# Where ScalarE scales the attention probabilities in the first mixer's loop, and what stands ahead of the copies

## The chip, the cores and the metric

The kernel is one program on one core of a Trainium2 chip. A core has five engines that each run their own list of instructions in order: TensorE (PE) multiplies and transposes, VectorE (DVE) and ScalarE (ACT) do elementwise work, GpSimd (POOL) helps, and SyncE (SP) issues the DMAs. They wait for each other by semaphores. The metric is the time of one execution in microseconds (us) on the device; smaller is better.

## The reference

Two blocks of two layers each run one after the other on 256 latent and 256 context tokens of width 1024. Only the mixer of the very first layer is touched. It joins two branches: a gated linear recurrence in two directions (four heads) and softmax attention (eight query heads, two key heads, 64 wide):

```
def _softmax_attend(q, k, v):
    s = jnp.einsum('bhgqd,bhkd->bhgqk', q, k, preferred_element_type=jnp.float32) * (ATT_HEAD_DIM ** -0.5)
    p = jax.nn.softmax(s, axis=-1).astype(v.dtype)
    return jnp.einsum('bhgqk,bhkd->bhgqd', p, v)
...
    o_lat = jnp.concatenate([a_lat, b_lat], axis=-1)
...
            w_out = even_w_out[j]
...
        x_lat = x_lat + m_lat[2] * _rms(o_lat @ w_out, norm_post_mix[l])
```

Latent queries see all 512 keys, context queries only the 256 context keys.

## The kernel before

The stage `Even` first projects the tokens, then runs a loop of 20 steps (`self.steps`). Each engine has its own copy of that loop (`pe`, `act`, `dve`), with the pieces of several pipelines written out by hand in the order in which that engine is to run them. Three pipelines are interleaved.

**Attention.** There are 16 units: four pairs of heads times four blocks of 128 queries. Unit t is started at step t + 2. Blocks 0 and 1 of a pair are context queries (256 keys wide), blocks 2 and 3 latent ones (512 wide), so units 2, 3, 6, 7, 10, 11, 14 and 15 are wide. For a unit, PE makes the scores of two heads (banks 3 and 4); DVE takes the maxima and scales them by -1/8 (`maxima`, lines 239 and 220); ACT takes the exponents with row sums (`exps`, line 263); DVE takes the reciprocals of the sums (`norms`, line 232); ACT multiplies the probabilities by them (`scale_act`, line 268, a copy with a scale); one step later PE turns the probabilities (`turn`, transposes at line 185, into bank 5) and ACT copies them out (`copy_one`, line 268); PE then multiplies by the values (`values`, one more step later). A wide unit is turned in two halves, head 0 and head 1, which share bank 5: the second turn waits for the first copy, and each `copy_one` waits for its turn. A narrow unit is turned and copied at once. In the loops, `t`, `t1` and `t2` are the units started in this step, one step ago and two steps ago.

**Recurrence.** In steps 0 to 13 (`halving`) a pair of heads goes through seven levels. Per level DVE makes differences (`split_dve`), ACT takes their exponents (`decay_act`, line 262, 128x1024, called E below), DVE multiplies by them (`queries_dve`, line 206, 128x1024), PE makes products, and DVE keeps a part of them under a mask (`keep`, line 245).

**Modulation rows.** PE multiplies two columns by 128x512 tiles of streamed weights (`mods.rows_pe`), which fill its gaps; the rows are copied by ACT (`mods.copy_act`, into `sb_RW`) and turned by PE (`mods.turn_pe`).

After the loop comes the output projection `OutProj`. Its first weights (`even_w_out`) are split for it by ACT (copy to `sb_WP`) and DVE; the first two pieces and the first blocks of the mixer's output (`sb_HP`) are already prepared in steps 17 to 19 (`EARLY`), at the end of ACT's step. PE starts its long run of `sb_HP`, `sb_WP` multiplies when its loop has ended.

Of ACT's three calls that matter, these lines say what each waits for:

```
    def exps(self, act, u):
...
        act.wait_ge("m", tag, u)
...
    def scale_act(self, act, u):
...
        act.wait_ge("recip", tag, u)
...
        act.wait_ge("tr", self.tag, u, h)
        act.copy(self.st["PT"][u % 2][:, h, 0:nk], self.p.ps[self.tb[0]][:, 0:nk]).then_inc(*act.sig("pt", self.tag, u, h))
```

Of the kernel before, what the change touches and what calls it, by code (L numbers as in the profile page):

```python
# [247 lines left out]
class Act(Engine):  # L248
# [8 lines left out]
    def act(self, out, a, func, scale=1.0, bias=0.0, accum=None):  # L257
        self.table(func)
        if self.e is None:
            return BLANK  # L260
        if accum is None:
            return self.e.activation(out, a, func, bias=bias, scale=scale)  # L262
        return self.e.activation(out, a, func, bias=bias, scale=scale, accum_out=accum)  # L263
# [138 lines left out]
class Start:  # L402
# [16 lines left out]
    def act(self, act):  # L419
        act = act.on(self.name)  # L420
        act.wait_ge("vec")
        act.act(self.e, self.src, ACT.Exp, scale=-1.0).then_inc(*act.sig("exp"))
# [20 lines left out]
class Mods:  # L443
# [60 lines left out]
    def col_copy_act(self, act, L):  # L504
        p, e = self.p, act.on(self.name(0))
        e.wait_ge("rows", L)
        e.copy(p.RW[:, 128 * L:128 * L + 128], p.ps[(7, 5)[L % 2]][:, 0:128]).then_inc(*e.sig("copied", L))
# [79 lines left out]
    def copy_act(self, act, r):  # L587

        p, e = self.p, act.on(self.name(r))
        e.wait_ge("rows", self.nq - 1)  # L590
        if self.before(r):
            e.wait_ge("turned", of=self.before(r))
        e.copy(p.RW[:, :], p.ps[7][:, :]).then_inc(*e.sig("copied"))
# [1996 lines left out]
class Even:  # L2590
# [301 lines left out]
    def act(self, act):  # L2892
        e = act.on("even.in")
        self.proj.act(e)
        act.fence("even.in")
        g, a, A = act.on("even.gla"), act.on("even.att"), self.attend
        for s in range(self.steps):
            t, t1, t2, n, n1 = self.unit(s), self.unit(s - 1), self.unit(s - 2), self.item(s), self.item(s - 1)
            mods, r, k = self.late_mods(s)
            if k == 4:  # L2900
                mods.copy_act(act, r)
            for x in n:
                self.square_act(a, x)
            for x in n1:
                self.root_act(a, x)
            if t1 is not None:
                A.copy_one(a, t1, 0)
            if t is not None:
                A.exps(a, t)
            if t2 is not None:  # L2910
                A.gather(a, t2)
            if self.halving(s):
                m, h = self.halving(s)
                self.levels[m].decay_act(g, h)
            self.linear_act(g, s)
            if t is not None:
                A.scale_act(a, t)
            if t1 is not None:
                A.copy_one(a, t1, 1)
            if s >= self.steps - 3:  # L2920
                self.out.some_act(act, *self.EARLY[s - self.steps + 3])
        self.out.act(act, 3, 5)
# [1922 lines left out]
```

## Time and profile before

| | |
|---|---|
| median of 3 runs | 2379.79 us (2375.83, 2379.79, 2380.3) |
| the profiled execution, its own time | 2374.38 us |
| its span in the trace | 2372.6 us |
| PE busy | 2219.6 us, 94% of the span |
| DVE busy | 1509.2 us, 64% |
| ACT busy | 1101.8 us, 46% |
| POOL busy | 127.5 us, 5% |
| the loop of the changed function in the trace | about 145 to 293 us |
| PE's run of the output projection behind it | 293.86 us on, 43.85 us |

Times of single instructions are read from the profiled execution. What lies outside its span is 1.8 us. A matmul that counts as busy may still be waiting inside the array, so a busy PE is not one at its peak; and a share of the whole span says nothing of a stage that is 6% of it.

### The profile page before, as it was taken

The page shows a single profiled execution, that of the slowest core. Times are in us where ns is not written, and L with a number is a line of the kernel's source. Part 1 is how long each engine was busy: PE and PEld are TensorE (multiplying, and loading weights), DVE is VectorE, ACT ScalarE, POOL GpSimd, SP SyncE. Part 2 cuts the span into 40 slices and gives each one's busy share as a digit, 9 for nine tenths or more (in the row PEclk, how much of TensorE's full clock was granted, in tenths as well). Part 3 has the DMA queues.
Part 4 walks back from the last instruction along what each step waited for, and adds up shares of the span by engine and source line. Part 5 has one row for each costly group of instructions (what it writes and reads, how often), then busy time and mean ns, then how long its engine had stood idle before and what let it go on. Part 6 is the DMA issues. An engine that isn't in the chain of part 4 may idle for free.

```text
span 2372.6 us, 34020 instructions
## 1 busy us (share of the span) xinstructions
PE 2219.6 (94%) x14120; PEld 1738.0 (73%) x14120; DVE 1509.2 (64%) x2424; ACT 1101.8 (46%) x1852; POOL 127.5 (5%) x171
## 2 busy tenths in 40 slices
PE   7987899999999999988999998999999998769999
PEld 5754468888886777776899863357888887669888
DVE  6477547565557577877777235555576576995665
ACT  5456634232226466655455345644232335445553
POOL 0000000000000000000010002201210111000210
PEclk9999999999999999999999999999999999989999
DMA  9253554444435554444654223442443435634553
GB/s 300 74 223 122 187 212 143 140 146 155 154 135 189 159 179 160 158 150 138 188 178 153 98 72 131 161 170 94 157 157 127 158 115 197 227 125 141 203 188 124
DMA packets 180747, 372.77 MB, mean 157 GB/s; under 512 B 7665, under 2 KB 108273, under 8 KB 167281
## 3 DMA queue, kind: packets, MB, share of 16 engines
q1 hardware_dynamic: 180592, 370.60, 45.1%
q8 instruction: 111, 1.82, 0.3%
q14 instruction: 44, 0.35, 0.0%
HBM read 340.14 MB, written 30.44 MB: 156 GB/s over the span
## 4 chain that ended last, share of the span: by engine, by line
PE 77%; DVE 12%; ACT 7%; issue 3%; SPq 1%; DMA 1%; POOL 0%; DVEq 0%; ACTq 0%; POOLq 0%
PE ps L169 75%; DVE sb_R L206 4%; ACT sb_R L262 2%; SPq L273 1%; PE ps L185 1%; DVE sb_H L206 1%; ACT sb_R L268 1%; DVE sb_WP L206 1%; DVE sb_R L239 1%; ACT sb_slot L268 1%; DVE sb_R L242 1%; DVE sb_X L223 1%; DVE sb_R L223 1%; ACT sb_R L263 0%; ACT L255 0%
## 5 line engine op out<-in xcount | busy, mean ns | idle before, releaser
L169 PE MATMUL ps<-sb_HP,sb_WP 128*128 128x512 f32 (+1 forms) x5200 | 1066.4, 365 | 12.5 <-DVE sb_HP L206 5.8
L169 PEld LDWEIGHTS ps<-sb_HP,sb_WP 128*128 128x128 f32 x5200 | 882.1, 189 | 180.4 <-issue 12.9
L206 DVE TENSOR_TENSOR sb_WP<-sb_slot,sb_WP 128x1024 fp32r<-128x1024 f32 x380 | 465.6, 1231 | 502.2 <-ACT sb_WP L268 501.6
L268 ACT ACTIVATE sb_WP<-sb_slot 128x1024 fp32r<-128x1024 f32 x380 | 398.7, 1056 | 667.7 <-PE ps L169 651.7
L169 PE MATMUL ps<-sb_XP,sb_WP 128*128 128x512 f32 (+1 forms) x2720 | 498.2, 345 | 0.7 <-DVE sb_R L236 0.3
L169 PEld LDWEIGHTS ps<-sb_XP,sb_WP 128*128 128x128 f32 x2720 | 432.8, 190 | 65.5 <-DVE sb_XP L206 1.6
L206 DVE TENSOR_TENSOR sb_R<-sb_R 128x256 f32<-128x256 f32 (+5 forms) x401 | 193.4, 517 | 10.3 <-ACT sb_R L262 6.7
L169 PE MATMUL ps<-sb_R 128*32 128x64 f32 (+7 forms) x1768 | 156.3, 293 | 31.6 <-DVE sb_R L206 7.1
L169 PEld LDWEIGHTS ps<-sb_R 128*32 128x32 f32 (+3 forms) x1768 | 109.7, 157 | 74.9 <-issue 38.4
L262 ACT ACTIVATE sb_R<-sb_R 128x512 f32<-128x512 f32 (+5 forms) x165 | 98.7, 600 | 120.8 <-DVE sb_R L206 78.5
L262 ACT ACTIVATE sb_R<-ps 128x512 f32<-128x512 f32 (+1 forms) x154 | 79.9, 558 | 89.1 <-PE ps L169 84.6
L206 POOL TENSOR_TENSOR sb_R<-sb_R 128x512 f32<-128x512 f32 (+1 forms) x68 | 67.3, 1013 | 723.9 <-ACT sb_R L262 512.9
L268 ACT ACTIVATE sb_R<-ps 128x512 f32<-128x512 f32 (+3 forms) x159 | 69.2, 514 | 56.6 <-PE ps L169 47.0
L169 PE MATMUL ps<-sb_WP,sb_HP 128*128 128x512 f32 x384 | 88.3, 391 | 1.3 <-DVE sb_HP L206 1.3
L169 PEld LDWEIGHTS ps<-sb_WP,sb_HP 128*128 128x128 f32 x384 | 71.9, 188 | 17.0 <-DVE sb_HP L206 1.7
L206 POOL TENSOR_TENSOR sb_H<-sb_H 128x512 f32<-128x512 f32 (+1 forms) x15 | 18.3, 1222 | 1108.4 <-ACT sb_H L262 1108.4
L169 PE MATMUL ps<-sb_H,sb_cst 128*128 128x512 f32 (+4 forms) x178 | 59.4, 474 | 19.7 <-ACT sb_H L262 15.5
L206 DVE TENSOR_TENSOR sb_cst<-sb_cst,sb_R 128x512 f32<-128x512 f32 (+1 forms) x112 | 69.6, 662 | 2.9 <-ACT sb_cst L262 2.5
L206 DVE TENSOR_TENSOR sb_XP<-sb_R,sb_XP 128x256 fp32r<-128x256 f32 (+1 forms) x116 | 69.4, 609 | 2.2 <-ACT sb_XP L268 1.6
L169 PEld LDWEIGHTS ps<-sb_H,sb_cst 128*128 128x128 f32 x178 | 30.4, 200 | 45.5 <-issue 19.5
L268 ACT ACTIVATE sb_slot<-ps 128x512 f32<-128x512 f32 (+3 forms) x112 | 43.5, 424 | 40.8 <-PE ps L169 21.4
L262 ACT ACTIVATE sb_H<-sb_X 128x512 f32<-128x512 f32 (+1 forms) x72 | 37.0, 531 | 52.5 <-DVE sb_X L223 34.8
(163 smaller groups left out, 1890.7 us busy)
## 6 DMA issues: line engine op xcount, KB each, us to landing
sb_slot<-mlp_w SPq DMA_DIRECT2D x32, 2048.0 KB, 7.6
sb_slot<-mod_w SPq DMA_DIRECT2D x12, 2048.0 KB, 7.5
sb_R<-ada_w SPq DMA_DIRECT2D x12, 2048.0 KB, 7.5
sb_slot<-ada_w SPq DMA_DIRECT2D x24, 1024.0 KB, 4.9
sb_slot<-ffn_w_gate SPq DMA_DIRECT2D x22, 1024.0 KB, 5.5
sb_slot<-ffn_w_up SPq DMA_DIRECT2D x22, 1024.0 KB, 8.0
sb_slot<-ffn_w_down SPq DMA_DIRECT2D x9, 2048.0 KB, 7.7
sb_slot<-odd_w_in SPq DMA_DIRECT2D x32, 512.0 KB, 7.1
```

The source lines that it names most:

```text
L169: return self.e.matmul(out, w, x, start=start, stop=stop, skip_group_check=True)
L185: return self.e.transpose(out, a, self.p.c("ident"))
L206: return BLANK if self.e is None else self.e.tensor_tensor(out, a, b, op)
L223: return BLANK if self.e is None else self.e.scalar_tensor_tensor(out=out, in0=a, scalar=s, in1=b, op0=op0, op1=op1)
L239: return BLANK if self.e is None else self.e.reduce_max(out, a, AX.X)
L242: return BLANK if self.e is None else self.e.tensor_tensor_scan(out, a, b, 0.0, ALU.mult, op)
L262: return self.e.activation(out, a, func, bias=bias, scale=scale)
L268: return self.e.activation(out, a, ACT.Copy) if scale is None else self.e.activation(out, a, ACT.Copy, scale=scale)
L273: return BLANK if self.e is None else self.e.dma_start(out, in_)
```

## The change

On ACT alone the order of three calls within a step is changed. The scaling of a unit moves from near the end of its own step to the head of the next one; and the exponents of this step's unit now stand ahead of the first copy of the turned unit of the step before.

```
--- before.py
+++ after.py
@@ -2899,22 +2899,22 @@
             mods, r, k = self.late_mods(s)
             if k == 4:
                 mods.copy_act(act, r)
+            if t1 is not None:
+                A.scale_act(a, t1)
             for x in n:
                 self.square_act(a, x)
             for x in n1:
                 self.root_act(a, x)
+            if t is not None:
+                A.exps(a, t)
             if t1 is not None:
                 A.copy_one(a, t1, 0)
-            if t is not None:
-                A.exps(a, t)
             if t2 is not None:
                 A.gather(a, t2)
             if self.halving(s):
                 m, h = self.halving(s)
                 self.levels[m].decay_act(g, h)
             self.linear_act(g, s)
-            if t is not None:
-                A.scale_act(a, t)
             if t1 is not None:
                 A.copy_one(a, t1, 1)
             if s >= self.steps - 3:
```

The instructions of PE, DVE, POOL and SP stand in the same order as before; no instruction is added or taken away on any engine.

On ACT around steps 5 and 6 (units 3 and 4; `sb_slot<-ps` is a copy of a turned unit, `sb_slot,sb_R<-ps,sb_R` the exponents, `sb_R<-sb_R 128x1024` is E, `sb_slot<-sb_slot,sb_R` the scaling, `sb_RW` the modulation rows), one piece of the difference:

```order
-L268 ACTIVATE sb_slot<-ps 128x512
 L263 ACTIVATE sb_slot,sb_R<-ps,sb_R 128x512 x2
-L262 ACTIVATE sb_R<-sb_R 128x1024
+L268 ACTIVATE sb_slot<-ps 128x512
+L262 ACTIVATE sb_R<-sb_R 128x1024
+L268 ACTIVATE sb_slot<-ps 128x512
+L268 ACTIVATE sb_RW<-ps 128x512
 L268 ACTIVATE sb_slot<-sb_slot,sb_R 128x512 x2
-L268 ACTIVATE sb_slot<-ps 128x512
-L268 ACTIVATE sb_RW<-ps 128x512
```

The first copy moved from ahead of the exponents to between them and E; the scaling moved behind the second copy and behind the copy of the modulation rows.

On ACT at the end of the loop (units 14 and 15, steps 17 to 19), as it was before:

```order
169 L263 ACTIVATE sb_slot,sb_R<-ps,sb_R 128x512 x2
170 L268 ACTIVATE sb_slot<-sb_slot,sb_R 128x512 x2
171 L268 ACTIVATE sb_slot<-ps 128x512
172 L268 ACTIVATE sb_WP<-sb_slot 128x1024 x2
173 L268 ACTIVATE sb_HP<-sb_H 128x512 x2
174 L268 ACTIVATE sb_RW<-ps 128x512
175 L268 ACTIVATE sb_slot<-ps 128x512 x2
176 L268 ACTIVATE sb_WP<-sb_slot 128x1024
```

and as it is now:

```order
170 L263 ACTIVATE sb_slot,sb_R<-ps,sb_R 128x512 x2
171 L268 ACTIVATE sb_slot<-ps 128x512 x2
172 L268 ACTIVATE sb_WP<-sb_slot 128x1024 x2
173 L268 ACTIVATE sb_HP<-sb_H 128x512 x2
174 L268 ACTIVATE sb_RW<-ps 128x512
175 L268 ACTIVATE sb_slot<-sb_slot,sb_R 128x512 x2
176 L268 ACTIVATE sb_slot<-ps 128x512 x2
177 L268 ACTIVATE sb_WP<-sb_slot 128x1024
```

The scaling of the last unit moved behind the first two copies to `sb_WP`, two to `sb_HP` and the one to `sb_RW`.

## Rows read from the trace of the kernel before

**Rows 1.** The page, first part: busy us (share), instructions by engine

```profile
PE 2219.6 (94%) x14120; PEld 1738.0 (73%) x14120; DVE 1509.2 (64%) x2424; ACT 1101.8 (46%) x1852; POOL 127.5 (5%) x171
```

**Rows 2.** Stretches: us from:to, length, busy by engine, PEclk, DMA share, GB/s

```profile
165.00:190.00 25.00, 17.89 (x140) 9.02 (x140) 23.91 (x49) 19.45 (x39) 0.00 (x0) 0.96 0.48 179
...
250.00:260.00 10.00, 7.66 (x61) 5.28 (x61) 4.91 (x10) 6.55 (x21) 0.00 (x0) 0.70 0.00 0
...
253.00:287.00 34.00, 30.99 (x238) 15.43 (x235) 7.97 (x18) 21.38 (x58) 0.00 (x0) 0.96 0.51 191
```

**Rows 3.** Timeline, ACT, step 5: start, us, what, [idle before <-releaser]

```profile
179.83 0.69 ACT L263 ACTIVATE sb_slot<-ps,sb_R 128x512 f32<-128x512 f32 x1 [1.67 <-DVE sb_R L220]
...
181.17 1.05 ACT L262 ACTIVATE sb_R<-sb_R 128x1024 f32<-128x1024 f32 x1
...
183.56 0.57 ACT L268 ACTIVATE sb_slot<-ps 128x512 f32<-128x512 f32 x1
```

**Rows 4.** Timeline, DVE, the same step

```profile
179.63 0.17 DVE L220 TENSOR_SCALAR sb_R<-sb_R 128x2 f32<-128x2 f32 x1
...
182.13 0.15 DVE L232 RECIPROCAL sb_R<-sb_R 128x2 f32<-128x2 f32 x1
182.33 1.23 DVE L206 TENSOR_TENSOR sb_R<-sb_R 128x1024 f32<-128x1024 f32 x1
```

**Rows 5.** Timeline, ACT, E of step 6, behind a narrow unit

```profile
188.68 1.06 ACT L262 ACTIVATE sb_R<-sb_R 128x1024 f32<-128x1024 f32 x1 [0.17 <-DVE sb_R L206]
```

**Rows 6.** Waits from 145 to 300 us: us in total, times, longest

```profile
ACT sb_slot L268 <- PE ps L185: 12.5, 15, 1.7
...
PE ps L169 <- DVE sb_slot L245: 10.6, 6, 2.9
...
PE ps L169 <- ACT sb_slot L263: 1.4, 1, 1.4
```

**Rows 7.** Timeline, PE, steps 12 and 13

```profile
254.50 1.12 PE L185 MATMUL ps<-sb_cst,sb_slot 128*128 128x128 f32 x4
...
257.34 0.66 PE L185 MATMUL ps<-sb_cst,sb_slot 128*128 128x128 f32 x4
```

**Rows 8.** Timeline, ACT, step 12

```profile
256.02 0.65 ACT L268 ACTIVATE sb_slot<-ps 128x512 f32<-128x512 f32 x1
```

**Rows 9.** Timeline, ACT, steps 17 to 19

```profile
285.58 1.33 ACT L268 ACTIVATE sb_slot<-sb_slot,sb_R 128x512 f32<-128x512 f32 x2 [0.23 <-DVE sb_R L232]
...
287.43 2.00 ACT L268 ACTIVATE sb_WP<-sb_slot 128x1024 fp32r<-128x1024 f32 x2
...
290.38 0.57 ACT L268 ACTIVATE sb_RW<-ps 128x512 f32<-128x512 f32 x1
290.86 0.58 ACT L268 ACTIVATE sb_slot<-ps 128x512 f32<-128x512 f32 x1
292.19 0.60 ACT L268 ACTIVATE sb_slot<-ps 128x512 f32<-128x512 f32 x1 [0.75 <-PE ps L185]
```

**Rows 10.** Timeline, PE, steps 17 to 19 and the output projection

```profile
284.81 0.66 PE L185 MATMUL ps<-sb_cst,sb_slot 128*128 128x128 f32 x4
287.55 0.63 PE L185 MATMUL ps<-sb_cst,sb_slot 128*128 128x128 f32 x4 [2.08 <-ACT sb_slot L268]
288.10 1.09 PE L169 MATMUL ps<-sb_slot,sb_R 128*64 128x128 f32 x16
291.01 0.66 PE L185 MATMUL ps<-sb_cst,sb_RW 128*128 128x128 f32 x4 [1.81 <-ACT sb_RW L268]
291.50 0.65 PE L185 MATMUL ps<-sb_cst,sb_slot 128*128 128x128 f32 x4
292.84 1.09 PE L169 MATMUL ps<-sb_slot,sb_R 128*64 128x128 f32 x16 [0.69 <-ACT sb_slot L268]
```

**Rows 11.** Timeline, PE, behind its longest idle time near 1030 us; and that stretch

```profile
1034.50 2.08 PE L169 MATMUL ps<-sb_R 128*128 128x128 f32 x8 [4.48 <-DVE sb_HP L229]
...
1034.00:1038.00 4.00, 3.50 (x14) 3.22 (x15) 4.00 (x10) 2.32 (x4) 0.00 (x0) 0.57 0.01 2
```

## What I expect before the run

> **What bounds the kernel now.** PE is busy for 94% of the span [rows 1], so for the whole program the question is whether PE starts something later or earlier. The loop that the change touches is looser than that, and I read it by stretches. From 165 to 190 us DVE is busy for 23.91 of 25 us and PE for 17.89: DVE sets the pace there. From 253 to 287 us PE has 30.99 of 34 us and DVE 7.97: there PE sets it [rows 2]. So I look for what the new order on ACT makes DVE wait for in the first part, and PE in the last.
>
> The timeline of one wide step shows how tightly ACT and DVE run side by side. Both start from the scaled maxima (179.63 to 179.80). ACT runs the two exponents from 179.83, then E from 181.17, which ends at 182.22 [rows 3]. DVE meanwhile makes differences, keeps products and takes the reciprocals, which end at 182.28, and multiplies by E from 182.33 [rows 4]. E is ready 0.11 us before that multiply: whatever is put ahead of E beyond 0.11 us, DVE waits for.
>
> **The change part by part.** No instruction is added or removed, so all costs are waits.
>
> *A, the first copy between the exponents and E.* A copy of a turned head holds ACT for 0.48 us from start to start (290.38 to 290.86 in [rows 9], a copy of the same 128x512 from PSUM). Before, it was done while ACT waited for the maxima (1.67 us of idle time ahead of the exponents in [rows 3]), so it cost nothing. Now that cover is gone: it lies behind the exponents and E starts 0.48 us later, less the 0.11 us of slack, some 0.37 us for DVE. The step shown is one of five in which E follows the exponents like this and DVE is waiting for it (units 2, 3, 7, 9, 10): 1.8 us. Behind a narrow unit E waits 0.17 us for DVE's differences anyway [rows 5], so between nothing and 0.31 us (0.48 - 0.17) is left; for the two such steps (units 1 and 4) I take 0.1 us each, since DVE comes later there. In the other steps E waits for a gather that waits for PE, or nobody waits for E. That DVE's delays reach PE is seen in the waits: PE waited six times, 10.6 us together, for the kept products of line 245 [rows 6]. A is 2.0 us. Bounds: nothing, if each delay is given back where DVE waits for PE; and 12 x 0.48 = 5.8 us, if each of the twelve E of the loop pays the whole copy.
>
> *B, the scaling behind the second copy.* The second copy waits for PE's second turn, which is nearly the last thing PE does in a step; the scaling then stands behind it, and PE's next first turn waits for the scaling. What covers this is PE's work at the head of a step, scores and modulation rows. Near 255 us: the turn of unit 10 started at 254.50 and took 1.12 us, the next unit's turn came at 257.34 [rows 7]; between them ACT's copy started at 256.02 [rows 8]. Two scalings take 1.33 us together [rows 9], a copy 0.6, so now the turn can start at 256.02 + 0.6 + 1.33 + 0.1 = 258.05, 0.7 us later. In the other steps the unit that is copied or the one that is scaled is narrow, which needs less, or the wide scores keep PE longer, and I count nothing. B is 0.7 us, from 0 to 1.5 (one more such step).
>
> *C, the end of the loop.* The largest single piece. Before, unit 15 was scaled at 285.58, before ACT turned to the output projection's weights. Now its scaling stands in the next step, behind two copies to `sb_WP`, which start only when those weights have landed (287.43), two to `sb_HP` and the copy to `sb_RW` [rows 9]. It starts where the first copy of unit 15 stood, at 290.86, and ends 1.33 us later, at 292.2. On PE the first turn of unit 15 ran at 287.55, and behind it, in order, the values of unit 14 (288.10), the turn of the modulation rows (291.01) and the second turn of unit 15 (291.50) [rows 10]. All four are now queued behind the wait for the scaling: turn at 292.3, values 0.55 later at 292.85, 1.02 us, rows' turn at 293.9, 0.48 us, second turn at 294.35 instead of 291.50. The copy (292.19), the values of unit 15 (292.84) and the output projection (293.86) follow as before. C is 2.85 us. It can't be much less, because all of it is one queue; bounds 2.1 (if the values of unit 14 cost nothing) and 3.3.
>
> *D, the clock behind the new gap.* PE's work of unit 14 ends at 285.47 (284.81 + 0.66) and its next turn would start at 292.3: 6.8 us of idle time where there were 2.08 [rows 10]. Behind the 4.48 us of idle time near 1030 us the granted clock was 0.57 over the next 4 us [rows 11], so part of what follows ran at the lower of the two levels (1.2 GHz). I expect the same here. What it costs is read from the turns: 1.12 us for four in the stretch with clock 0.70, 0.66 otherwise [rows 2, 7]. The chain from the turn of unit 15 to the values of unit 15 holds 0.55 + 1.02 + 0.48 + 0.48 + 1.02 = 3.55 us of PE work; at 1.7 times that is 2.5 us more if all of it runs slow, and with a few matmuls of the projection 3. I take the middle, 1.3 us; bounds 0 (the loss falls into waits) and 3.
>
> A page of the Trainium skill bears on D: "TensorE: Matmul & The Clock Gate", section "Part 4: PE-mode transpose", says that transposes do not count as PE work in the same way and that the full clock does not engage for them. The rows show transposes of one shape at both durations, so they do follow the clock; whether they count is shown by no run here. By that page the turns would not help to bring the clock back, and the sum would be 8.6 us instead of 6.9.
>
> *Gains.* Exponents no longer stand behind a copy that waits for PE (12.5 us in 15 waits [rows 6]). In eight of these steps ACT then had to wait for the maxima anyway. Who would use earlier exponents? The reciprocals and through them the scaling, which now stands later in the queue; and the next scores, which waited for their bank once, 1.4 us [rows 6]. I count nothing.
>
> The sum: 2.0 + 0.7 + 2.85 + 1.3 = 6.9 us. PE runs the output projection without a gap behind it (43.85 us), all later loads and stages start from it, so I see nothing downstream that takes it back.
>
> **The rivals.**
>
> 1. *The loop hides A and B.* PE-bound stretches stand behind the DVE-bound ones; if the delays all end in DVE's waits for PE, only C and part of D are left, 2.9 to 4.7 us. For it: DVE is idle for long in 253 to 287 us. Against it: PE waited for DVE six times before that.
> 2. *The end is hidden too.* If the gap at the end had another cause that moves (the landing of the weights sets the start of the projection, not unit 15), C would vanish: 0 to 2 us. Against it: in the trace the last thing before the projection is the values of unit 15, which waited for ACT's copy.
> 3. *Faster.* Earlier exponents let reciprocals, scores and the pace of the step come earlier. It is worth at most the 12.5 us of those 15 waits [rows 6]. Against C alone (2.85 us) and the 4.8 us that a measurement needs, some 7.7 of them must arrive at PE; with all of them the time is 2377.6 + 2.85 - 12.5 = 2368 us, with 7.7 it is 2372.8. The rows show one wait of PE for exponents, 1.4 us.
> 4. *The clock stays low through the whole tail*: D is 3 instead of 1.3, the sum 8.6 us. For it: the gap is longer than the one near 1030 us. Against it: PE has work in between. It is what the page above would give.
>
> **How the numbers follow.** The sum stands against the profiled execution, 2374.4 us; the three runs have their median 5.4 us above it and spread over 4.5 us. The four executions average 2377.6 us, and from there I go: 2377.6 + 6.9 = 2384.5 us. About 0.2% (4.8 us) is what a measurement of this kernel can tell from no change.
>
> Chances: the sum with a middling clock 0.47, with a low one (rival 4) 0.15, rival 1 0.22, rival 2 0.10, rival 3 0.06. Slower by over 0.2%: the first two and a small part of rival 1, less what the spread of the runs takes away, 0.63. Within: 0.31. Faster: 0.06. For the range: rival 1 from the average gives 2380.5, from the profiled execution 2377.3; the top is the low clock with A and B near 3.5 and 1.0, from the median, 2379.8 + 3.5 + 1.0 + 2.85 + 3 = 2390. I give 2378 to 2390. Within it the sum's own range is 2381 to 2389.
>
> **What would show it.** A: in the wide steps up to 250 us E starts 0.48 us behind the end of the exponents, with the copy between, and the 128x1024 multiply of DVE waits for line 262. B: the first turn of unit 11 waits for line 268. C: the scaling of unit 15 stands behind `sb_RW`; PE is idle for about 7 us before its first turn, and the projection starts 5.5 to 8 us later than at 293.86 counted from the start of the loop. D: the granted clock is below 1 behind that gap. I would be wrong if DVE's multiply waited no longer than before, if the projection started within 2 us of its old place, or if the stages behind it took the delay back; and a clock that falls elsewhere, or no longer falls between 250 and 260 us, could cover the sum.

## The result and the profile after

The changed kernel takes 2385.62 us (median of 13 runs, 2381.95 to 2389.31), the kernel before 2379.79 us in 13 runs beside it (2375.83 to 2382.96). The ratio is 1.0024, 95% interval 1.0017 to 1.0032: it is some 5.8 us slower. The profiled execution took 2387.95 us, 2.3 us above its own median, and the one of before lies 5.4 us below its median; so single places of the two traces are compared here, not their spans.

The first lines of the page, span and busy time by engine:

```profile
span 2386.2 us, 34012 instructions
...
PE 2227.4 (93%) x14120; PEld 1740.8 (73%) x14120; DVE 1509.8 (63%) x2424; ACT 1101.1 (46%) x1852; POOL 127.5 (5%) x171
```

As many matmuls as in [rows 1], but PE is busy for 7.8 us more, at a mean granted clock of 0.978 where it was 0.982. This is not the change's alone: runs 1 and 4 below, which leave the scalings where they were, have PE busy for 2231.6 and 2229.5 us with the same matmuls. DVE's and ACT's busy times are those of before within 0.7 us. No work was added, so what was lost is waits and clock.

ACT in step 5 and the beginning of step 6 (start, duration, what, idle time before):

```profile
179.21 0.69 ACT L263 ACTIVATE sb_slot<-ps,sb_R 128x512 f32<-128x512 f32 x1 [2.18 <-DVE sb_R L220]
179.89 0.68 ACT L263 ACTIVATE sb_slot<-ps,sb_R 128x512 f32<-128x512 f32 x1
180.55 0.59 ACT L268 ACTIVATE sb_slot<-ps 128x512 f32<-128x512 f32 x1
181.03 1.06 ACT L262 ACTIVATE sb_R<-sb_R 128x1024 f32<-128x1024 f32 x1
182.30 0.60 ACT L268 ACTIVATE sb_slot<-ps 128x512 f32<-128x512 f32 x1 [0.21 <-PE ps L185]
182.79 0.59 ACT L268 ACTIVATE sb_RW<-ps 128x512 f32<-128x512 f32 x1
183.27 1.33 ACT L268 ACTIVATE sb_slot<-sb_slot,sb_R 128x512 f32<-128x512 f32 x2
```

DVE in step 5, its multiply by E:

```profile
182.19 1.23 DVE L206 TENSOR_TENSOR sb_R<-sb_R 128x1024 f32<-128x1024 f32 x1 [0.53 <-ACT sb_R L262]
```

E stands 0.48 us behind the copy's start, which is now ahead of it, and the multiply, which waited for nothing in [rows 4], waits 0.53 us for line 262. Counted from the first exponent, E started at 1.34 us in [rows 3] and starts at 1.82 us here.

PE's timeline around the same place:

```profile
182.19 0.70 PE L169 MATMUL ps<-sb_R 64*128 64x256 f32 x4
184.66 0.66 PE L185 MATMUL ps<-sb_cst,sb_slot 128*128 128x128 f32 x4 [1.76 <-ACT sb_slot L268]
```

The scores of step 6 are narrow and take PE 0.70 us. In that time ACT has to make the second copy, the copy to `sb_RW` and both scalings; the turn behind the scores waits 1.76 us for them. At the same place of the trace before it was 0.76 us:

```profile
184.28 0.63 PE L185 MATMUL ps<-sb_cst,sb_slot 128*128 128x128 f32 x4 [0.76 <-ACT sb_slot L268]
```

One step on, the turn of unit 4 waits too, behind scores that are again narrow and a scaling that is narrow:

```profile
194.59 0.70 PE L169 MATMUL ps<-sb_R 64*128 64x256 f32 x4
196.14 0.66 PE L185 MATMUL ps<-sb_cst,sb_slot 128*128 128x128 f32 x4 [0.84 <-ACT sb_slot L268]
```

In the trace before the same turn (at 193.90) waits for nothing.

PE's and DVE's waits from 145 to 306 us, by what was waited for (us in total, times, longest):

```profile
PE ps L185 <- ACT sb_slot L268: 19.3, 10, 7.8
...
DVE sb_R L206 <- ACT sb_R L262: 8.6, 8, 4.3
...
ACT sb_WP L268 <- DMA sb_slot<-even_w_out: 2.4, 1, 2.4
```

The first two rows in the trace before, of the same stretch (the third has none there):

```profile
PE ps L185 <- ACT sb_slot L268: 9.7, 8, 2.1
...
DVE sb_R L206 <- ACT sb_R L262: 5.1, 2, 4.3
```

Each has more short waits now, and the first has one long one, at the end of the loop. ACT there, in its timeline:

```profile
293.66 2.00 ACT L268 ACTIVATE sb_WP<-sb_slot 128x1024 fp32r<-128x1024 f32 x2 [2.41 <-DMA sb_slot<-even_w_out]
295.57 1.13 ACT L268 ACTIVATE sb_HP<-sb_H 128x512 fp32r<-128x512 f32 x2
296.61 0.57 ACT L268 ACTIVATE sb_RW<-ps 128x512 f32<-128x512 f32 x1
297.09 1.32 ACT L268 ACTIVATE sb_slot<-sb_slot,sb_R 128x512 f32<-128x512 f32 x2
```

and PE in the same time:

```profile
289.97 0.66 PE L185 MATMUL ps<-sb_cst,sb_slot 128*128 128x128 f32 x4
298.47 1.11 PE L185 MATMUL ps<-sb_cst,sb_slot 128*128 128x128 f32 x4 [7.84 <-ACT sb_slot L268]
299.51 1.98 PE L169 MATMUL ps<-sb_slot,sb_R 128*64 128x128 f32 x16
301.42 1.12 PE L185 MATMUL ps<-sb_cst,sb_RW 128*128 128x128 f32 x4
302.33 0.71 PE L185 MATMUL ps<-sb_cst,sb_slot 128*128 128x128 f32 x4
303.72 1.09 PE L169 MATMUL ps<-sb_slot,sb_R 128*64 128x128 f32 x16 [0.69 <-ACT sb_slot L268]
304.74 7.55 PE L169 MATMUL ps<-sb_HP,sb_WP 128*128 128x512 f32 x32
```

Unit 15's scaling waits behind the weights' landing and the five copies, and PE is idle for 7.84 us ahead of its turn. What follows the idle time takes 1.11 and 1.98 us, where the same instructions took 0.63 and 1.09 in [rows 10]. The granted clock says the same (stretch, length, busy by engine, PEclk, DMA share, GB/s):

```profile
288.00:295.00 7.00, 2.62 (x24) 1.18 (x23) 3.21 (x6) 3.66 (x8) 0.00 (x0) 1.00 0.92 342
295.00:300.00 5.00, 1.53 (x10) 1.21 (x11) 3.31 (x4) 3.80 (x7) 0.00 (x0) 0.57 0.58 236
```

A yardstick for this place is used below: from the start of the first `sb_WP` copy to the start of the projection. Here it is 304.74 - 293.66 = 11.08 us; in the profile before 293.86 - 287.43 = 6.43 us. Here that copy waits 2.41 us for its weights. In the profile before it waits for nothing that the trace shows: it starts at 287.43, and the second copy of unit 14, which ACT does just before, ends at 287.40:

```profile
286.83 0.57 ACT L268 ACTIVATE sb_slot<-ps 128x512 f32<-128x512 f32 x1
```

In the profiles of all eight runs below it waits, 1.0 to 2.5 us, also in those that leave unit 15's scaling in its place. It starts 2.5 to 3.9 us behind the start of unit 14's second turn, in no relation to that place (2.51 in run 3 and 3.87 in run 1, which leave it; 3.84 in run 5, which moves it). So this wait is more likely a matter of the single execution than of the order on ACT; one profile of each kernel doesn't show it. The yardstick starts behind it. The first of these transfers is issued 4.7 to 5.3 us ahead of the second turn of unit 14 in all ten profiles: a loop that is later makes the weights later too.

### The profile page after: what moved, and what is told of

Same layout as the page of the kernel before. It is cut to its first block, busy times and chain, and to the rows that moved or that the text cites. A ratio compares the mean times of both kernels' runs of the same rounds, so it can differ in the third digit from the quotient of the medians.

```text
span 2386.2 us, 34012 instructions
## 1 busy us (share of the span) xinstructions
PE 2227.4 (93%) x14120; PEld 1740.8 (73%) x14120; DVE 1509.8 (63%) x2424; ACT 1101.1 (46%) x1852; POOL 127.5 (5%) x171
## 3 DMA queue, kind: packets, MB, share of 16 engines
q8 instruction: 111, 1.82, 0.3%
## 4 chain that ended last, share of the span: by engine, by line
PE 74%; DVE 16%; ACT 6%; issue 2%; SPq 1%; DMA 1%; POOL 0%; DVEq 0%; ACTq 0%; POOLq 0%
PE ps L169 73%; DVE sb_R L206 7%; DVE sb_R L242 2%; ACT sb_R L262 2%; SPq L273 1%; DVE sb_H L206 1%; PE ps L185 1%; DVE sb_R L239 1%; DVE sb_WP L206 1%; DVE sb_X L223 1%; DVE sb_R L223 1%; ACT sb_R L268 1%; ACT sb_slot L268 1%; ACT sb_R L263 0%; ACT L255 0%
## 5 line engine op out<-in xcount | busy, mean ns | idle before, releaser
L169 PE MATMUL ps<-sb_slot,sb_SX 128*2 128x512 f32 (+1 forms) x504 | 59.5, 560 | 1.1 <-DMA sb_slot<-mod_w 1.1
```

The costliest lines, as they stand in the source:

```text
L169: return self.e.matmul(out, w, x, start=start, stop=stop, skip_group_check=True)
```

## The experiments

Eight kernels, in two groups of four; each group shares its runs of the kernel before (2380.1 us, then 2379.68 us, 35 runs each). Each was timed in 11 or 12 runs, and an interval of one ratio is some 0.2% (4 to 5 us) wide. Most of these intervals overlap, so the times say which kernels are slower than before and hardly rank the terms; the traces size them, each from one execution.

**1. Only the exponents are moved** (A alone):

```
+            if t is not None:
+                A.exps(a, t)
             if t1 is not None:
                 A.copy_one(a, t1, 0)
-            if t is not None:
-                A.exps(a, t)
```

Expected: 

> The scaling stays in its old place; only the exponents go ahead of the first copy, so that the copy stands between them and E. If the copy ahead of E is a real cost (A), DVE's 128x1024 multiply waits about 0.5 us for line 262 in the wide steps and the kernel is 2 to 3.5 us slower than before, with the end of the loop unchanged (PE idle about 2 us ahead of the first turn of unit 15). If the loop hides this (rival 1), it is within 1 us of before.

Measured: 2381.85 us, ratio 1.0011 (1.0002 to 1.002), 1.8 us slower, just under the 2 to 3.5 us expected. DVE waits for line 262 as in the changed kernel; its row in the waits of this run, 145 to 306 us:

```profile
DVE sb_R L206 <- ACT sb_R L262: 8.6, 8, 4.3
```

That is 3.5 us of waits more than before, for 1.8 us of time by the medians. The end of the loop was not as in the profile before: the `sb_WP` copy waits 2.44 us for the weights, the turn of unit 15 only 0.91 us, and the turn of the modulation rows, whose copy stands behind the weights, far longer:

```profile
295.49 0.71 PE L185 MATMUL ps<-sb_cst,sb_RW 128*128 128x128 f32 x4 [4.22 <-ACT sb_RW L268]
...
297.77 1.97 PE L169 MATMUL ps<-sb_slot,sb_R 128*64 128x128 f32 x16 [0.69 <-ACT sb_slot L268]
```

The values multiplies of unit 15, 1.09 us in [rows 10], take 1.97 us here, though no scaling was moved.

**2. Only the scalings are moved** (B, C and D; the copy stays ahead of the exponents):

```
+            if t1 is not None:
+                A.scale_act(a, t1)
...
-            if t is not None:
-                A.scale_act(a, t)
```

Expected: 

> The copy stays ahead of the exponents; only the scaling moves to the head of the next step. If the sum of the prediction holds, this carries B, C and D: 4 to 5.5 us slower than before, PE idle for about 7 us ahead of the first turn of unit 15 and a clock that falls behind it. If most of the loss is the copy ahead of E, it is at most 2 us slower. If what is measured is only clocks that fall by chance, it is within 1 us of before.

Measured: 2385.04 us, ratio 1.0016 (1.0007 to 1.0026), 4.9 us slower. DVE's waits for line 262 are those of before (5.1 us, 2 times). PE's row in the waits of this run, of the same stretch:

```profile
PE ps L185 <- ACT sb_slot L268: 17.2, 11, 7.2
```

The turn that corresponds to the one at 196.14 waits 0.85 us (at 198.41). By the medians most of the loss is in the scalings; the intervals of runs 1 and 2 overlap.

**3. The changed kernel with unit 15 scaled in its own step** (without C and D):

```
-            if t1 is not None:
+            if t1 is not None and t1 != 15:
                 A.scale_act(a, t1)
...
             self.linear_act(g, s)
+            if t == 15:
+                A.scale_act(a, t)
```

Expected: 

> The changed kernel, but unit 15 alone is scaled at the end of its own step as before. If C and D are what the prediction says, it is 4 us faster than the changed kernel and 2 to 3 us slower than before (A and B stay), and the gap of PE ahead of the first turn of unit 15 is again about 2 us. If the loop hides A and B (rival 1), it is within 1 us of before. If the end costs nothing (rival 2), it is as slow as the changed kernel, 5 to 6 us over before.

Measured: 2384.0 us, ratio 1.0017 (1.0007 to 1.0026): 3.9 us above before and only 1.6 below the changed kernel, where 4 were expected. In its trace the long idle time is gone (0.98 us ahead of the first turn of unit 15, where about 2 were expected), but another of 2.80 us is left, ahead of the turn of the modulation rows, whose copy to `sb_RW` stands behind the `sb_WP` and `sb_HP` copies as it always did. The yardstick is 297.80 - 290.48 = 7.32 us, 3.8 below the changed kernel's. So the end was shortened as expected in the trace and by less in the times. The intervals of this kernel and of the changed one overlap and rule out neither 1.6 nor 4 us; run 5 tries the end by itself.

**4. The kernel before, with E directly behind the exponents** (the reverse of A, with the old scalings):

```
-            if t1 is not None:
-                A.copy_one(a, t1, 0)
             if t is not None:
                 A.exps(a, t)
+            if self.halving(s):
+                m, h = self.halving(s)
+                self.levels[m].decay_act(g, h)
+            if t1 is not None:
+                A.copy_one(a, t1, 0)
             if t2 is not None:
                 A.gather(a, t2)
-            if self.halving(s):
-                m, h = self.halving(s)
-                self.levels[m].decay_act(g, h)
```

Expected: 

> The kernel before, but with E ahead of the first copy and of the gather: exponents, E, copy, gather, and the scaling in its old place. If what the change loses in the loop is the copy ahead of E, this loses nothing: from 2 us faster than before (E no longer waits for a gather that waits for PE) to the same time. If instead the loss comes from the copy being later than before, whatever it stands behind, PE's second turn waits for it and this is 2 to 4 us slower than before.

Measured: 2379.55 us, ratio 0.9997 (0.9988 to 1.0007). DVE's waits for line 262 fall to 0.8 us, also the longest one, of 4.3 us, where E had stood behind a gather. The time does not move: 4.3 us of DVE's waits went away, and the median is 0.6 us lower, which the interval can't tell from nothing. As the copy and the gather also come later here, the run doesn't price that wait alone.

**5. The kernel before, with only unit 15's scaling moved** (C and D alone):

```
-            if t is not None:
+            if t is not None and t != 15:
                 A.scale_act(a, t)
...
                 mods.copy_act(act, r)
+            if t1 == 15:
+                A.scale_act(a, t1)
```

Expected: 

> Only the scaling of unit 15 is moved to the head of the next step; all else is the kernel before. It isolates terms C and D. By the prediction (2.85 + 1.3) it is 3 to 4.5 us slower than the kernel before, PE is idle for about 7 us before the first turn of unit 15 and the projection starts 4 us later counted from the landing of its weights. If the landing of the weights hides the end (rival 2, and what the small gain of the kernel with unit 15 put back suggests) it is 0 to 2 us slower, with a shorter idle time of PE or the same start of the projection.

Measured: 2382.77 us, ratio 1.0011 (1.0002 to 1.002), 3.1 us slower, at the lower end of what the prediction's terms give and above rival 2. PE's timeline of this run at the end:

```profile
293.84 1.12 PE L185 MATMUL ps<-sb_cst,sb_slot 128*128 128x128 f32 x4 [7.98 <-ACT sb_slot L268]
294.88 1.98 PE L169 MATMUL ps<-sb_slot,sb_R 128*64 128x128 f32 x16
...
299.44 1.97 PE L169 MATMUL ps<-sb_slot,sb_R 128*64 128x128 f32 x16 [0.69 <-ACT sb_slot L268]
301.35 10.91 PE L169 MATMUL ps<-sb_HP,sb_WP 128*128 128x512 f32 x43
```

One scaling out of 16 makes the whole idle time. The yardstick is 301.35 - 289.04 = 12.31 us, 5.9 us above before where 4 were expected, with both values multiplies at the lower clock (1.98 and 1.97 us).

**6. The changed kernel, with E ahead of the first copy** (takes A away; exponents, E, copy, gather as in 4, with the scalings of the changed kernel).

Expected: 

> The changed kernel with E put directly behind the exponents, ahead of the first copy and the gather. It takes term A away from the changed kernel. If A is worth 2 us there, the time is 2 us below the changed kernel, some 2383.5 us, and DVE's 128x1024 multiply hardly waits for line 262 (below 1 us in all, where it waited 8.6 us). If A ends in waits of DVE for PE, the waits go and the time stays within 1 us of 2385.6 us.

Measured: 2384.7 us, ratio 1.0016 (1.0008 to 1.0025), 0.9 us below the changed kernel by the medians, within the 1 us of the second expectation. The waits for line 262 are 0.8 us; as in run 4, the one behind the gather is gone with the others. By this run A is worth less than by the first; the times can't tell 1 us from 2.

**7. The changed kernel, with PE kept at work in its idle time** (takes D away). The seven matmuls are extra work whose results nobody reads:

```
             if mods and q < 4 and not whole:
                 mods.rows_pe(pe, r, q, (0,))
+            if t1 == 15:
+                b = A.sb[0]
+                a.vacant(b)
+                for _ in range(7):
+                    a.mm(A.p.ps[b][:, 0:512], A.p.c("ident"), A.p.cst[:, 0:512], True, True)
             if t1 is not None:
                 A.turn(a, t1, 0)
```

Expected: 

> The changed kernel with seven matmuls (128x512, results read by nobody) put on PE ahead of the first turn of unit 15, into a score bank that is free then. PE works through most of its idle time; the moment at which unit 15's scaling is ready does not move. If the clock falls because of the idle time (term D), the turns behind it take 0.66 us instead of 1.11, the values of unit 14 1.1 instead of 1.98, and the time is 1.3 to 2.5 us below the changed kernel. If the clock falls for another reason, or costs nothing there, the time is that of the changed kernel within 1 us and the turns are as slow as before.

Measured: 2383.7 us, ratio 1.0016 (1.0007 to 1.0025), 1.9 us below the changed kernel by the medians. PE's timeline of this run at the end:

```profile
287.82 6.17 PE L169 MATMUL ps<-sb_cst 128*128 128x512 f32 x14
295.39 0.66 PE L185 MATMUL ps<-sb_cst,sb_slot 128*128 128x128 f32 x4 [1.40 <-ACT sb_slot L268]
295.98 1.09 PE L169 MATMUL ps<-sb_slot,sb_R 128*64 128x128 f32 x16
297.00 0.66 PE L185 MATMUL ps<-sb_cst,sb_RW 128*128 128x128 f32 x4
297.50 0.60 PE L185 MATMUL ps<-sb_cst,sb_slot 128*128 128x128 f32 x4
298.78 1.09 PE L169 MATMUL ps<-sb_slot,sb_R 128*64 128x128 f32 x16 [0.69 <-ACT sb_slot L268]
299.81 12.54 PE L169 MATMUL ps<-sb_HP,sb_WP 128*128 128x512 f32 x54
```

and the stretch behind the filled time, beside the same of the changed kernel above (0.57):

```profile
295.00:300.00 5.00, 3.92 (x45) 3.18 (x46) 0.54 (x2) 2.80 (x5) 0.00 (x0) 1.00 0.04 15
```

With PE at work the clock stays at 1.00 and each instruction has its short duration again. The four profiles that have the long idle time (7.17 to 7.98 us: the changed kernel, runs 2, 5 and 6) all show the turn behind it at 1.11 or 1.12 us and the values at 1.98. The yardstick is 299.81 - 290.59 = 9.22 us. This run takes the end apart: 9.22 - 6.43 = 2.79 us above before is the queue (C), and what is above 9.22 in the others is the clock (D): 11.08 - 9.22 = 1.86 us in the changed kernel, 12.31 - 9.22 = 3.09 us in run 5, and by the same yardstick (304.39 - 293.84 = 10.55 and 300.79 - 288.47 = 12.32) 1.33 us in run 2 and 3.10 in run 6. That the time itself falls is not shown: the ratios of this run and of the changed kernel (1.0017 to 1.0032) overlap.

**8. Run 4 with the copy to `sb_RW` ahead of the `sb_WP` copies**, an attempt at a better version, from what run 3 showed:

```
-            if k == 4:
+            if k == 4 and s != self.steps - 2:
                 mods.copy_act(act, r)
...
+            if s == self.steps - 3:
+                mods, r, k = self.late_mods(s + 1)
+                mods.copy_act(act, r)
             if s >= self.steps - 3:
                 self.out.some_act(act, *self.EARLY[s - self.steps + 3])
```

Expected: 

> The kernel with E directly behind the exponents and all scalings in their old place, and besides the copy to sb_RW put ahead of the two sb_WP copies, where ScalarE waits 1.72 us for the weights. By the chain of the tail (PE waits 3.5 us for that copy, and the second copy of unit 15 then follows the first directly) the projection starts 1.3 us earlier, counted from the landing of its weights, than in the same kernel without it, so 2378 us against 2379.55; if the idle time of 3.5 us was also what lowered the clock there, up to 3 us are gained. If the weights alone set the start, nothing is gained.

Measured: 2380.74 us, ratio 1.0002 (0.9992 to 1.0012). The rows' turn no longer waits and the yardstick is 6.29 us against 7.51 in run 4, 1.2 us less where 1.3 were expected. Only 0.5 us of that is the order: the second turn of unit 15 starts 3.57 us behind the start of the `sb_WP` copy (293.38 - 289.81), where it was 4.07 (294.18 - 290.11). The rest is that this turn and the values behind it took 0.66 and 1.44 us here, 0.85 and 1.97 in run 4. PE now waits 3.32 us for the first copy of unit 15, and the time shows no gain. No version here beats the kernel before.

## Why the prediction was right

The sum was 6.9 us; measured are 5.8 us. The start of 2377.6 us was 2.2 us too low, the sum 1.1 us too high, and the two errors partly cancel in 2384.5 against 2385.62 us: that the total came this close is in part luck. It is not faster, the end is not hidden (run 5: 3.1 us by the medians), and A and B are not hidden in the loop, since the changed kernel without the end's loss (run 3) is still 3.9 us slower. Rival 4, the low clock through the whole tail, is what the profiles of runs 5 and 6 show, and half of it what the changed kernel's does. One sign was too low: the projection was to start 5.5 to 8 us later, counted from the start of the loop, and starts 10.9 us later (304.74 against 293.86, the loops starting within 0.04 us). A single pair of traces can't be read so closely: in run 4, whose time is that of before, it starts 3.8 us later (297.62).

**A (2.0 us).** The mechanism is as told: the copy ahead of E, and DVE waiting for line 262. Each wait was 0.1 to 0.2 us longer than the 0.37 us estimated, and there were six such steps, not five: unit 11 (at 257.18), where nobody was thought to wait for E, has one too. At 250.39 a wait of 0.39 us behind line 232 became one of 0.88 us for line 262, which counts 0.49 us: 0.51 + 0.53 + 0.53 + 0.58 + 0.49 + 0.54 = 3.2 us. The two narrow steps have none. By the medians 1.8 us of these waits reached the time in run 1 and 0.9 us in run 6, neither of them sharp.

**B (0.7 us).** This is the term that was mis-sized, and its place was mostly wrong. The first turn of unit 11 waits for nothing in the changed kernel's trace (at 262.43). There the scores ahead of it took 1.23 us; in runs 2, 3, 6 and 7, where they took 0.70, it waits 0.30 to 0.43 us for line 268, but so it does in run 5, without B (0.52). The step that failed is "in the other steps the unit that is copied or the one that is scaled is narrow, which needs less, or the wide scores keep PE longer". In step 6 the unit copied and scaled is wide, the copy to `sb_RW` stands between, and the scores that should cover it are narrow (0.70 us): the turn waits 1.00 us longer than before. In step 7 the unit scaled is narrow, and the turn at 196.14 still waits 0.84 us where it waited for nothing. These two are B's: all five kernels with the scalings moved have them (1.24 to 1.76 and 0.84 to 0.85 us), and those that scale in the old place have not (0.69 to 0.77 us in before, run 1 and run 5, nothing in runs 4 and 8; and nothing in all five at the second place). Of the other waits that grew, the one at 243.90 (1.67 against 0.86 us) belongs to both parts, as run 1 has 1.19 and run 2 has 1.21 there; those at 231.56 (1.00 against 0.60) and 251.21 (1.53 against 1.25) are not B's, as run 2 has 0.51 and 1.26. So B is some 1.8 to 2.7 us of waits (1.84 us in the two steps, up to 0.81 more at 243.90). In time, run 2 less run 5 (4.9 - 3.1) gives 1.8 us and run 3 less run 1 (3.9 - 1.8) 2.1 us, differences with an uncertainty of some 3 us.

**C (2.85 us).** Right in place and size: 2.79 us by run 7's yardstick, and the order on ACT is the one told. One reading in it was not: at 287.43 the trace before shows no wait for the weights. Where they are waited for, PE's idle time is longer than forecast (7.84 us instead of 6.8), and the queue behind them is as long as it was summed to be. So the landing does set when the tail starts in nine of the ten profiles, as rival 2 had it, and it hides nothing, because the scaling stands behind it.

**D (1.3 us, 0 to 3).** Right in cause: in run 7's trace, with PE at work, the clock does not fall. That the time falls with it (1.9 us by the medians) is inside the noise. Its size differs between executions, 1.3 to 3.1 us in those profiled; in the changed kernel the second turn (0.71 us) and the last values (1.09) were fast again, in run 5 they were not (1.06 and 1.97). What the turns by themselves do for the clock's return is shown by no run, since values multiplies always stand among them. Kernels that scale unit 15 in its own step pay for the clock there as well: in the profiles of runs 1, 3 and 4 the turn of the rows waits 4.22, 2.80 and 3.50 us for `sb_RW`, and the last values take 1.97 or 1.98 us. The kernel before has the same tail, so its one profile (no wait for the weights, all at 1.00) is probably a favourable one, and that may be why C and D, 5.9 us by the yardstick in run 5's profile (12.31 - 6.43), are 3.1 us in its times. That last part is argued, not shown: the kernel before has no second profile.

**Gains.** None were counted, and run 1, which has only the earlier exponents and A, is 1.8 us slower. Whether a small gain is hidden in it, the times can't tell.

What stays open is the share of each term in the time: taken alone they are 1.8 (A), 1.8 to 2.1 (B) and 3.1 us (C and D), about 7 in sum, against 5.8 together. An overlap of 1 us and the scatter of the runs explain that equally well.

## What to carry to other kernels

In a loop that several engines run in lockstep, a move by a few places in one engine's list is costed by what stands ahead of it in every step, also the rare ones: here a copy of modulation rows that comes every sixth step, and above all the last steps, where the list holds preparations for the next stage that wait for a DMA. Check the cover of a moved instruction step by step with the sizes of both units involved, since wide and narrow ones alternate and the cover belongs to another unit than the work. And when one term is an idle time of PE, cost the slower matmuls behind it too, and compare with more than one execution of the kernel before.

## What was not expected of the hardware

The clock takes a different course behind nearly the same idle time: after 7.84 us of it PE's granted clock was 0.57 from 295 to 300 us and the work from 302.33 on ran at its short durations, while after 7.98 us in run 5 the values at 299.44 still took 1.97 us, and a stretch of run 5 reads (columns as above)

```profile
293.00:301.00 8.00, 6.48 (x44) 5.42 (x44) 1.32 (x3) 3.59 (x7) 0.00 (x0) 0.50 0.06 23
```

that is, the lower level throughout, with PE busy for 6.48 of 8 us. The other two are divided in the same way: after 7.17 us (run 2) the turn of the rows at 301.59 took 0.66 us again, after 7.36 us (run 6) the values at 298.88 still took 1.97 us. What decides between the two courses is not shown by these runs.
